# The second rotary attention's product with v, four blocks in one visit instead of two, and the mask ahead of the scores in its PSUM bank

## The reference

```python
s = jnp.einsum('bnqhgd,bnchd->bnhgqc', q, kb).astype(jnp.float32) * (d ** -0.5)
mask = (jnp.abs(kpos - qpos) <= WINDOW) & (kpos >= 0) & (kpos < S)
s = jnp.where(mask[None, :, None, None], s, -jnp.inf)
m = jnp.maximum(jnp.max(s, axis=-1, keepdims=True), sink)
e = jnp.exp(s - m)
pr = e / (jnp.sum(e, axis=-1, keepdims=True) + jnp.exp(sink - m))
o = jnp.einsum('bnhgqc,bnchd->bnqhgd', pr.astype(v.dtype), vb).reshape(B, S, Hq * d)
```

## Time and profile before

| | |
|---|---|
| median of 3 runs | 1026.41 us (1026.39 to 1027.71) |
| the profiled execution | 1027.09 us |
| its span, first to last instruction | 1025.0 us |
| mean granted TensorE clock | 0.999 of full |
| PE busy | 1016.2 us, 99% |
| DVE busy | 778.1 us, 76% |
| ACT busy | 610.5 us, 60% |

### The profile page before, as it was taken

The page is one execution under the profiler, slowest core; times in us unless marked ns, Lnnn a source line. Parts: engine busy times, 40 slices in busy tenths (PEclk is TensorE's granted clock), DMA queues, the critical chain, the costliest instruction groups (busy, mean ns, idle before and its releaser), DMA issues.

```text
span 1025.0 us, 15564 instructions
## 1 busy us (share of the span) xinstructions
PE 1016.2 (99%) x5912; PEld 870.9 (85%) x5912; DVE 778.1 (76%) x1106; ACT 610.5 (60%) x935; POOL 40.5 (4%) x74
## 2 busy tenths in 40 slices
PE   9999999999999999999999999999999999999997
PEld 7777888888888877788888888899899978888886
DVE  6987678988887787869988887866667677655654
ACT  6677766666656768767656566734454755444443
POOL 1000010000000000000000000500000000000000
PEclk9999999999999999999999999999999999999999
DMA  8643345655644551536665646565453356565541
GB/s 314 214 147 123 124 165 186 226 177 192 204 164 174 177 184 43 184 125 198 213 196 173 205 164 205 175 192 170 147 180 126 125 184 206 180 213 181 177 150 42
DMA packets 114784, 177.42 MB, mean 173 GB/s; under 512 B 3436, under 2 KB 85797, under 8 KB 114725
## 3 DMA queue, kind: packets, MB, share of 16 engines
q1 hardware_dynamic: 113460, 173.67, 51.0%
q10 hardware_dynamic: 1264, 2.95, 0.8%
HBM read 175.56 MB, written 1.05 MB: 172 GB/s over the span
## 4 chain that ended last, share of the span: by engine, by line
PE 96%; DMA 2%; DVE 1%; issue 0%; ACT 0%; POOL 0%; POOLq 0%; DVEq 0%; ACTq 0%
PE ps L1952 92%; DMA raw<-in_diff_w_qkv 2%; PE ps L2060 1%; PE ps L2472 1%; PE ps L2106 1%; PE ps L2614 0%; PE ps L2224 0%; PE ps L2545 0%; DVE wlo L1230 0%; ACT whi L640 0%; PE ps L2244 0%; DVE h L1911 0%; DVE wlo L1247 0%; DVE xs L1297 0%; PE ps L2189 0%
## 5 line engine op out<-in xcount | busy, mean ns | idle before, releaser
L1230 DVE TENSOR_TENSOR wlo<-raw,whi 128x2048 fp32r<-128x2048 f32 x147 | 335.4, 2287 | 73.5 <-ACT whi L640 73.2
L1952 PE MATMUL ps<-xs,whi 128*128 128x512 f32 (+1 forms) x1536 | 336.3, 352 | 0.0
L640 ACT ACTIVATE whi<-raw 128x2048 fp32r<-128x2048 f32 x147 | 279.2, 1909 | 41.1 <-PE ps L1952 30.5
L1952 PEld LDWEIGHTS ps<-xs,whi 128*128 128x128 f32 x1536 | 267.4, 189 | 39.4 <-issue 2.1
L1952 PE MATMUL ps<-xs,wlo 128*128 128x256 f32 x1248 | 202.4, 283 | 0.0
L1952 PE MATMUL ps<-whi,xs 128*128 128x512 f32 (+1 forms) x576 | 182.0, 393 | 0.9 <-DVE whi L1508 0.4
L1952 PEld LDWEIGHTS ps<-xs,wlo 128*128 128x128 f32 x1248 | 175.2, 191 | 2.9
L1952 PEld LDWEIGHTS ps<-whi,xs 128*128 128x128 f32 x576 | 106.6, 188 | 24.3 <-issue 2.9
L1952 PE MATMUL ps<-whi,ohi 128*128 128x512 f32 (+1 forms) x370 | 126.0, 397 | 0.0
L1952 PE MATMUL ps<-whi,olo 128*128 128x512 f32 (+1 forms) x370 | 123.2, 389 | 0.0
L1952 PE MATMUL ps<-wlo,ohi 128*128 128x512 f32 (+1 forms) x370 | 123.0, 389 | 0.0
(11 more groups left out here) (194 smaller groups left out, 960.4 us busy)
## 6 DMA issues: line engine op xcount, KB each, us to landing
raw<-in_ffn_w_up SPq DMA_DIRECT2D x44, 1024.0 KB, 5.1
raw<-in_w_in SPq DMA_DIRECT2D x23, 1024.0 KB, 5.3
raw<-in_ffn_w_down SPq DMA_DIRECT2D x22, 1024.0 KB, 4.8
raw<-in_w_mlp_in SPq DMA_DIRECT2D x16, 1024.0 KB, 5.3
raw<-in_w_mlp_out SPq DMA_DIRECT2D x16, 1024.0 KB, 4.9
raw<-in_diff_w_qkv SPq DMA_DIRECT2D x11, 1024.0 KB, 5.3
raw<-in_ple_w_gate SPq DMA_DIRECT2D x8, 1024.0 KB, 5.0
raw<-in_swa_w_qkv SPq DMA_DIRECT2D x6, 1024.0 KB, 5.2
```

The lines of the kernel that those rows point to most:

```text
L640: act.activation(whi[:, u % RING, :], raw[:, u % RAW, :], ACT.Copy).then_inc(hi_ready, 1)
L1230: dve.tensor_tensor(wlo[:, u % RING, :], raw[:, u % RAW, :], whi[:, u % RING, :].bitcast(F32), ALU.subtract).then_inc(lo_ready, 1)
L1952: return pe.matmul(o, l, r, start=start, stop=stop, skip_group_check=True)
```

## The change

`pv1` is called in passes 2, 6 and 10 and in wo_rest, for four blocks at a time: s - 2 to s + 1. It fills all four quarters of bank OB. `swa_hi` and `swa_lo` move with it and take 512 columns at once; `o_ready` and `o_read` step by 4. Since the transposed probabilities of four blocks have to last until then, ATs gets a second buffer, used by alternate passes. In `scores1` the two mask matmuls are put ahead of the scores: the mask opens the bank, the scores are added to it, and `s_ready` is raised by the last score matmul of each bank.

```diff
-        ATs = region(9216, 1024, "p (b k c) -> p b k c", b=2, k=4)
+        ATs = [region(first, 1024, "p (b k c) -> p b k c", b=2, k=4) for first in (9216, 2560)]
...
 (ScalarE)
                 def swa_hi(s):
-                    g, qt, _, i = SWA_BLOCKS[s]
-                    m = 4 * g + i // 2
-                    act.wait_ge(o_ready, S_AT["1"] + s + 2)
-                    act.activation(ohi[:, m:m + 3:2, qt * P:(qt + 1) * P], ps[:, OB, 0:2 * P].rearrange("p (a c) -> p a c", c=P),
+                    g, qt, _, _ = SWA_BLOCKS[s]
+                    act.wait_ge(o_ready, S_AT["1"] + s + 4)
+                    act.activation(ohi[:, 4 * g:4 * g + 4, qt * P:(qt + 1) * P], ps[:, OB, :].rearrange("p (a c) -> p a c", c=P),
                                    ACT.Copy).then_inc(swa_hi_ready, 1)
...
-                    copy_T(ATs[:, 0].rearrange("p k c -> p (k c)"), ps[:, TB, :])
+                    copy_T(ATs[s // 2 % 2][:, 0].rearrange("p k c -> p (k c)"), ps[:, TB, :])
...
-                    swa_hi(s)
+                    if s % 4 == 2:
+                        swa_hi(s - 2)
...
 (VectorE)
-                    dve.wait_ge(swa_hi_ready, s // 2 + 1)
-                    dve.tensor_tensor(olo[:, m:m + 3:2, qt * P:(qt + 1) * P], ps[:, OB, 0:2 * P].rearrange("p (a c) -> p a c", c=P),
-                                      ohi[:, m:m + 3:2, qt * P:(qt + 1) * P].bitcast(F32), ALU.subtract).then_inc(o_read, 2)
+                    dve.wait_ge(swa_hi_ready, s // 4 + 1)
+                    dve.tensor_tensor(olo[:, 4 * g:4 * g + 4, qt * P:(qt + 1) * P], ps[:, OB, :].rearrange("p (a c) -> p a c", c=P),
+                                      ohi[:, 4 * g:4 * g + 4, qt * P:(qt + 1) * P].bitcast(F32), ALU.subtract).then_inc(o_read, 4)
...
-                    swa_lo(s)
+                    if s % 4 == 2:
+                        swa_lo(s - 2)
...
 (TensorE)
                     pair = [ps[:, 6 + r, :].rearrange("p (j c) -> p j c", j=2) for r in range(2)]
+                    for r in range(2):
+                        mm(pair[r][:, :, c:c + P], identb[:, :], maskb[:, qt, :].unsqueeze(1).broadcast_to([P, 2, P]), True, False)
                     for j in range(2):
                         for r in range(2):
                             rows_ = slice(r * HD, (r + 1) * HD)
-                            mm(pair[r][:, j, :], qS[rows_, 4 * g + i + j, qt * P:(qt + 1) * P], kT[rows_, g, :], j == 0, False)
-                    for r in range(2):
-                        mm(pair[r][:, :, c:c + P], identb[:, :], maskb[:, qt, :].unsqueeze(1).broadcast_to([P, 2, P]), False, True)\
-                            .then_inc(s_ready, 1)
+                            ins = mm(pair[r][:, j, :], qS[rows_, 4 * g + i + j, qt * P:(qt + 1) * P], kT[rows_, g, :], False, j == 1)
+                            if j == 1:
+                                ins.then_inc(s_ready, 1)
...
                 def pv1(s):
                     pe.wait_ge(o_read, S_AT["1"] + s)
-                    for n in (s, s + 1):
+                    for n in range(s, s + 4):
                         g, qt, r, i = SWA_BLOCKS[n]
+                        a = i // 2 + 2 * r
                         c = (2 * g + r) * HD
                         pe.wait_ge(t_free, T_USE[f"1A{n}"] + 1)
                         for k in range(2):
                             for j in range(2):
-                                ins = mm(ps[j * HD:(j + 1) * HD, OB, r * P:(r + 1) * P], vtm[:, k, c:c + HD],
-                                         ATs[:, n % 2, 2 * j + k, :], k == 0, k == 1)
-                    ins.then_inc(o_ready, 2)
+                                ins = mm(ps[j * HD:(j + 1) * HD, OB, a * P:(a + 1) * P], vtm[:, k, c:c + HD],
+                                         ATs[n // 2 % 2][:, n % 2, 2 * j + k, :], k == 0, k == 1)
+                    ins.then_inc(o_ready, 4)
...
-                    pv1(s)
+                    if s % 4 == 2:
+                        pv1(s - 2)
...
-                               (2, lambda: pv1(2 * N_A - 2)),
+                               (2, lambda: pv1(2 * N_A - 4)),
```

More of the change, by code:

```diff
@@ L1027, in _ @@
                         split_half()
-                    copy_T(ATs[:, 1].rearrange("p k c -> p (k c)"), ps[:, TB, :])
+                    copy_T(ATs[s // 2 % 2][:, 1].rearrange("p k c -> p (k c)"), ps[:, TB, :])
                     if more:
```

## The result

The changed kernel takes 1028.63 us (median of 22 runs, 1027.86 to 1029.34), the kernel before, run beside it, 1026.76 us (22 runs). The ratio is 1.0018, 95% interval [1.0013, 1.0024]: slower by 1.87 us. The forecast was +1.06 us. It had the sign, the stretch and the kind of loss, and fell short of the size. The upper end of its range was 1028.6 us, 0.03 us under what was measured.

The account below looks back on a forecast made before the run. TensorE, busy 99% of the span, was taken as the bound. Pass pairs, waits against saved visits, summed to +0.91 us; unhidden weight loads added +0.15: +1.06, or 1027.5 us, called the same; range 1025.0 to 1028.6 us.

Parts of the forecast that it names:

- A visit's price: Product with v on TensorE: getting into and out of the two column tiles costs 0.36 us each time; four fewer save 1.44.
- The short passes wait: Passes without the product: TensorE, with 3.22 us of work left, idles about 0.45 us before probs_T1(2), (10) and (14).
- the last of the first bank two records earlier: Scores in passes 8 and 12: mask first releases the first block's maximum 0.19 us earlier, since its last score record starts earlier.
- X: Start of a pass's second group of transposes, probs_T1(s + 1); in pass 0 it is 1.82 us after the pass began.
- The rival of the deeper waits: Passes 8 and 12 get no mask help (+0.38 us), the end loses its cover (+0.47): 1028.3 us, still the same; chance 0.11.
- the start behind a wait: Pass 0: probs_T1(2) can't start before X + 3.68, about 0.05 us after VectorE's scaling ends at X + 3.63.
- transposes behind row tiles: Transposes now directly following the scores: extra cost taken as 0, bounds -0.22 and +0.20 us a visit, times 8.
- the slower rival: Transposes right behind row tiles pay 0.20 us for their weight load at each of eight visits: 1029.1 us; chance 0.13.
- Pass 4: probs_T1(6) waits for ScalarE's q copy, then piece1(6) for ple_proj; with pass 6 +0.59 us, said to hold most of the loss.
- The evacuations: Wider pair at the end: 0.47 us longer together, but covered by the residual sum's 0.67 us wait for TensorE, so nothing.

## Why the prediction was right or wrong

- **A visit's price was right.** With two visits fewer and hardly any waits the two pairs took 12.19 and 12.18 us against 12.53, 0.35 less each, forecast 0.36 (the whole stretch 0.63 less). The Trainium skill (TensorE: Matmul & The Clock Gate, Part 2) has a drain of about 128 cycles; the estimate from two of them, 0.11 us, is a third of what the kernel pays.
- **The short passes wait: right.** The idle times came at probs_T1(2), (10) and (14), ended by VectorE's multiplication, as forecast. The first two go when their pass is lengthened, and those of passes 8 and 12 shrink when VectorE's queue is relieved.
- **What failed first: "the last of the first bank two records earlier", the 0.19 us that the mask first was to bring passes 8 and 12.** It spaced the eight records evenly, 0.106 us apart, which put the last one of the first bank 0.54 us before X. They start in pairs, one record on each row tile, and both banks' last ones start 0.31 us before X. So the first increment comes at X + 0.08 and not 0.14 before X; with the mask last it comes at X + 0.07. The maxima start 0.10 us after X with the mask first, 0.09 with the mask last, and X to the next pass is 3.98 us both ways. I had 3.69. This is 2 x 0.19 = 0.38 us of the miss. The rival of the deeper waits had this term; its other one, 0.47 us at the end, did not come.
- **The second: the start behind a wait, X + 3.68.** I took 0.05 us from a VectorE end to the matmul (the row used gives 0.06), and 0.05 more for the weight load. It is 0.14 us (381.01 to 381.15), 0.09 above the 0.05, at three places 0.27 us, of which 0.15 had been in the sum. The row used was of another form. These transposes wait for two semaphores, `scaled_e` and the bank's `t_free`, and in the packed trace the wait for `scaled_e` is an instruction of its own (381.04 to 381.09) ahead of the weight load at 381.12. The matmul of the row used has none between its release and its weight load. Nor has the one that waits at piece1(5), and that too starts 0.06 us after its release (393.22 to 393.28). That this instruction is the cause is not shown: no run took the second wait away.
- **The third: transposes behind row tiles, where I took 0** between bounds of -0.22 and +0.20. They cost 0.06 us, the figure I had seen behind column tiles and argued away. It is paid in the passes that don't wait, and it also makes the evacuation start 0.05 us later in pass 0. The two increments on row tiles need not be in it: the column tiles carry a single one and have the same 0.06. It was not the 0.12 us from which the slower rival decides, and there are seven such places in the loop and not eight.
- **Pass 4: the size right (+0.63 measured for the pair, +0.59 forecast), the wait wrong.** I put it at probs_T1(6), behind ScalarE's copy. It came earlier, at piece1(5), which waits for rope_read, and VectorE's rope_sin ends at 392.48 + 0.74 = 393.22, 0.06 us ahead of it. I had not looked at what piece1(4) and piece1(5) wait for. The run with the rope work earlier shows that both queues hold TensorE by nearly the same time, so that either alone gives nearly the same loss. So the size came out right by luck: the limit I had worked out stands just behind the one that acted. "Most of the loss" it was not, but a third.
- **The evacuations: right.** The residual sum at the end still waits 0.18 us for TensorE (0.67 before), so 0.49 us of the cover are used up, 0.47 was reckoned:

```profile
428.60 0.69 DVE L1288 TENSOR_TENSOR h<-ps,h 128x512 f32<-128x512 f32 x1 [0.18 <-PE ps L1952]
```

By pairs: 0/2 +0.32 (forecast 0.10), 4/6 +0.63 (0.59), 8/10 +0.50 (0.11), 12 and the end +0.42 (0.11), together 1.87. Of the 0.81 us beyond the forecast 0.38 is the mask that didn't help and 0.12 the start behind a wait. Of the other 0.31 the rows place 0.29. In passes 2 and 10 it is 1.98 us from the second transposes to the visit, and was 1.93: 0.10. The transposes that waited are 1.84 to 1.86 us ahead of the next ones, where it was 1.82: 0.09. In pass 0 the scaling ends at X + 3.69 and not X + 3.63: 0.06. And 0.04 is the miss of passes 4 and 6.

## What to carry to other kernels

When work is taken out of one turn of a loop and put into the next, the bound engine gains only if each turn is still longer than the chain on the other engines that leads from it to the next. Here TensorE had 3.22 us of work where the chain took 3.83 to 3.99. First put other work into the emptied turn and reorder the other engines' queues to match, then merge; done so for two pairs, with the mask last, the merge gained 0.63 us, where in the changed kernel with the mask last the same two pairs had lost 0.67 (12.77 and 12.96 us against 12.53). And read every wait of a group that will come earlier, not only the one next to the edit.

## What the runs showed of the hardware

Matmuls on two row tiles, issued one after the other into two banks, start 7 ns apart and raise their semaphore 0.04 us apart (404.304 and 404.346): the first bank's reader started no earlier for having its last matmul issued ahead of the other's. Transposes directly behind row-tiled matmuls are busy 0.66 us for four in place of 0.60, the same as behind column tiles. A group of fp32 transposes that waited for VectorE starts 0.14 us after the end of the instruction it waited for, its weight load 0.11 us after, with a wait instruction of its own between, where a matmul of 512 columns without one had started after 0.06. Two visits to two column tiles made into one, with all their records kept, took off 0.35 us.
